# Carried part of a gated recurrence: two 64x64 products per chunk become one 128x128 product on zero-padded states

## What is computed

```python
b = jnp.cumsum(log_f, axis=3)                       # within a chunk
scores = jnp.einsum('bhntd,bhnsd->bhnts', q * jnp.exp(b - b_mid), k * jnp.exp(b_mid - b))
o_intra = jnp.einsum('bhnts,bhnse->bhnte', jnp.where(lower, scores, 0.0), v)
contrib = jnp.einsum('bhnsd,bhnse->bhnde', k * jnp.exp(b_last - b), v)
decay = jnp.exp(b_last[:, :, :, 0, :])
def step(state, inp):
    dec, add = inp
    return dec[..., None] * state + add, state
_, states_in = lax.scan(step, zeros, (decay, contrib))
o_inter = jnp.einsum('bhntd,bhnde->bhnte', q * jnp.exp(b), states_in)
return o_intra + o_inter
```

## Time and profile before

| | |
|---|---|
| Median of 3 runs | 1178.36 us (1177.79 to 1179.91) |
| Profiled execution | 1178.43 us, span from first to last instruction 1176.6 us |
| Busy | PE 99%, PEld 80%, DVE 54%, ACT 38%, POOL 9% |
| Chain that ended last | PE 97%, DVE 1%, ACT 1%, DMA 1% |
| L1414, the carried products | 224 records, 2% of the chain |
| L1040, the scans of states | 8, 1.21 us each |

### The profile page before, as it was taken

One profiled execution on the slowest core, in us unless ns is written; L12 is line 12 of the kernel. 1 busy time (PEld: TensorE's weight loads), 2 busy tenths in 40 slices (PEclk: granted clock), 3 DMA queues, 4 the chain that ended last, 5 costly groups with the idle time before them and its releaser, 6 DMA issues.

```text
span 1176.6 us, 15837 instructions
## 1 busy us (share of the span) xinstructions
PE 1166.8 (99%) x5988; PEld 943.1 (80%) x5988; DVE 636.1 (54%) x768; ACT 445.6 (38%) x650; POOL 100.7 (9%) x82
## 2 busy tenths in 40 slices
PE   9999999999999999999999999999999999999997
PEld 7888888888888777777777778888888888888886
DVE  6755555543334674444599965756455555552223
ACT  6423322322223445455755534444332332231223
POOL 0000000000001210000165510011000000000000
PEclk9999999999999999999999999999999999999999
DMA  6333233233224231111131112422323323323221
GB/s 202 108 107 101 79 105 107 94 132 99 98 78 177 83 124 55 59 67 55 36 108 38 48 61 72 171 98 90 102 95 107 106 77 102 107 80 118 90 90 72
DMA packets 31678, 111.64 MB, mean 95 GB/s; under 512 B 3984, under 2 KB 5136, under 8 KB 31376
## 3 DMA queue, kind: packets, MB, share of 16 engines
q1 hardware_dynamic: 30192, 104.11, 26.5%
q10 hardware_dynamic: 1440, 6.88, 1.6%
HBM read 105.48 MB, written 4.19 MB: 93 GB/s over the span
## 4 chain that ended last, share of the span: by engine, by line
PE 97%; DVE 1%; ACT 1%; DMA 1%; issue 0%; ACTq 0%; SPq 0%; DVEq 0%
PE ps L1124 26%; PE ps L1125 25%; PE ps L1126 25%; PE ps L1160 3%; PE ps L1158 3%; PE ps L1159 3%; PE ps L1414 2%; PE ps L1264 1%; PE ps L1273 1%; PE ps L1289 1%; PE ps L1409 1%; PE ps L1393 1%; PE ps L1374 1%; PE ps L1194 0%; PE ps L1197 0%; DMA raw<-gates_dram 0%
## 5 line engine op out<-in xcount | busy, mean ns | idle before, releaser
L1124 PE MATMUL ps<-h_hi,w_hi 128*128 128x512 f32 x1024 | 407.5, 398 | 0.0
L1126 PE MATMUL ps<-h_hi,w_lo 128*128 128x512 f32 x1024 | 399.0, 390 | 0.0
L1125 PE MATMUL ps<-h_lo,w_hi 128*128 128x512 f32 x1024 | 399.0, 390 | 0.0
L741 DVE TENSOR_TENSOR w_lo<-raw,w_hi 128x1024 fp32r<-128x1024 f32 (+2 forms) x190 | 233.6, 1232 | 193.6 <-ACT w_hi L411 187.9
L411 ACT ACTIVATE w_hi<-raw 128x1024 fp32r<-128x1024 f32 (+1 forms) x182 | 196.2, 1080 | 174.4 <-PE ps L1126 96.1
L1124 PEld LDWEIGHTS ps<-h_hi,w_hi 128*128 128x128 f32 x1024 | 192.2, 188 | 56.0 <-issue 17.0
L1125 PEld LDWEIGHTS ps<-h_lo,w_hi 128*128 128x128 f32 x1024 | 192.3, 188 | 41.3 <-issue 2.9
L1126 PEld LDWEIGHTS ps<-h_hi,w_lo 128*128 128x128 f32 x1024 | 192.2, 188 | 41.0
L481 ACT ACTIVATE g_hi<-un 128x512 f32 (+1 forms) x44 | 27.8, 632 | 250.8 <-DVE un L741 250.8
L741 DVE TENSOR_TENSOR un<-ps,rs 128x512 f32<-128x512 f32 x44 | 30.4, 691 | 122.2 <-PE ps L1126 122.2
L1124 PE MATMUL ps<-g_hi,w_hi 128*128 128x512 f32 x176 | 68.5, 389 | 0.0
(11 more groups left out here) (233 smaller groups left out, 1237.7 us busy)
## 6 DMA issues: line engine op xcount, KB each, us to landing
raw<-up_dram SPq DMA_DIRECT2D x86, 512.0 KB, 3.2
raw<-proj_dram SPq DMA_DIRECT2D x26, 512.0 KB, 3.3
raw<-down_dram SPq DMA_DIRECT2D x16, 704.0 KB, 4.1
raw<-down_dram SPq DMA_DIRECT2D x22, 512.0 KB, 3.2
raw<-gates_dram SPq DMA_DIRECT2D x16, 512.0 KB, 3.2
raw<-branch_dram SPq DMA_DIRECT2D x8, 512.0 KB, 3.3
raw<-wout_dram SPq DMA_DIRECT2D x8, 512.0 KB, 3.2
x_spill_dram<-xT ACTq DMA_DIRECT2D x1, 2048.0 KB, 7.3
```

The lines of the kernel that those rows point to most:

```text
L741: return V.tensor_tensor(out, a, b, op)
L1124: T.matmul(ps[:, bank, :], w_hi[:, slot, cols], moving_hi(j), start=start and j == 0, stop=False)
L1125: T.matmul(ps[:, bank, :], w_hi[:, slot, cols], moving_lo(j), start=False, stop=False)
L1126: ins = T.matmul(ps[:, bank, :], w_lo[:, slot, cols], moving_hi(j), start=False, stop=stop and j == tiles - 1)
```

## The change

The carried product is made for both heads at once. For that each state has 128 columns in place of 64, [128, 128, 8]: rows 0 to 63 hold the first head's state in columns 0 to 63, rows 64 to 127 the second head's in columns 64 to 127, and the rest is zero. The product of such a state with the queries of both heads gives both outputs, one above the other. The zeros are written once, by two memsets of POOL ahead of `to_end(0)`, behind waits for the last silu, the attention's last transposes and products, and the spill. `state[0]` stays in its place and takes the place of the old `state[1]` too, which now lies in tiles 6 and 7 of `xT`. As the two heads' states no longer lie in the same columns, the scan becomes two scans of 64 partitions each, and the waits for `state_done` count two for each unit.

```diff
-        state = [at("state0", 84, [P, HD, NSUP]), at("state1", 86, [P, HD, NSUP])]
+        state = [at("state0", 84, [P, 2 * HD, NSUP])[:], xT[:, 6:8, :].rearrange("p a (e n) -> p (a e) n", n=NSUP)]
...
             key(0)
             key(1)
+            pool.wait_ge(sil_done, HH)
+            pool.wait_ge(pt_done, 2 * ITEMS)
+            pool.wait_ge(pv_done, ITEMS)
+            pool.wait_ge(spilled, 16)
+            for padded in state:
+                nc.gpsimd.memset(padded, 0.0).then_inc(pad_zeroed, 1)
             to_end(0)
...
                 if u >= 2:
-                    act.wait_ge(state_done, u - 1)
+                    act.wait_ge(state_done, 2 * (u - 1))
...
-                con, flat = ps[:, 4 + u % 2, :], state[u % 2][:].rearrange("p e n -> p (e n)")
-                V.tensor_tensor_scan(flat[:, turn], decay[u % 2][:, turn], con[:, turn], 0.0, ALU.mult, ALU.add).then_inc(state_done, 1)
+                con = ps[:, 4 + u % 2, :]
+                if u < 2:
+                    dve.wait_ge(pad_zeroed, 2)
+                for a, rows in enumerate(head_rows):
+                    flat = state[u % 2][rows, HD * a:HD * (a + 1), :].rearrange("p e n -> p (e n)")
+                    V.tensor_tensor_scan(flat[:, turn], decay[u % 2][rows, turn], con[rows, turn], 0.0,
+                                         ALU.mult, ALU.add).then_inc(state_done, 1)
...
-                pe.wait_ge(state_done, u + 1)
+                pe.wait_ge(state_done, 2 * u + 2)
...
-                        for rows in head_rows:
-                            ins = T.matmul(ps[rows, 7, cc], state[d][rows, :, n + 1 if d else n - 1], b_cum[u % 3][rows, cc],
-                                           start=False, stop=d == 1 and n == NSUP - 2)
+                        ins = T.matmul(ps[:, 7, cc], state[d][:, :, n + 1 if d else n - 1], b_cum[u % 3][:, cc],
+                                       start=False, stop=d == 1 and n == NSUP - 2)
```

More of the change, by code:

```diff
@@ L216, in build @@
         o_done, osq_done, oms_done = sem("o_done"), sem("osq_done"), sem("oms_done")
+        pad_zeroed = sem("pad_zeroed")
         oeps_done, or_done, on_done, ybhi_done, yblo_done = (sem(n) for n in (
@@ L229, in build @@
         RAW_CREDIT, W_CREDIT, BANK_CREDIT = RAW_SLOTS, W_SLOTS, 2
+        head_rows = (slice(0, HD), slice(HD, P))
         block = ctx.enter_context(nc.Block())
@@ L1346, in _ @@
                 gate_unit(g)
-            head_rows = (slice(0, HD), slice(HD, P))
             def mean_square(t):
@@ L1389, in contributions @@
                 if u >= 2:
-                    pe.wait_ge(state_done, u - 1)
+                    pe.wait_ge(state_done, 2 * (u - 1))
                 for j in range(ST):
```

## The result

The changed kernel takes 1207.44 us (median; 1206.75 to 1209.81), the kernel before beside it 1178.29: ratio 1.0249, 95% interval 1.0238 to 1.0261. It is slower, as forecast, but by 29.1 us and not by 13.4, and so outside the range that ended at 1194.0. The profiled execution took 1207.81 us, its span is 1205.9.

What follows compares the result with a forecast made beforehand. TensorE (PE), busy for 99% of the span, was taken to bound the kernel. 1178.4 + 13.4 (carried products) + 0 (scans) + 0 (zeroing) = 1191.8 us, range 1183.8 to 1194.0.

Steps and rivals of the forecast that it cites:

- PE bounds, the recurrence has no waits to swallow anything: Recurrence: PE busy for all 109.00 us, one 0.6 us wait from 600 us on; added PE time lengthens the kernel.
- The two heads' products run side by side, so halving the records saves nothing: Carried products in `outputs(u)`: both heads' products start together, so rounds stay 112 and the tempting 10 us is not there.
- A round is the strided load, and it goes by columns: Carried products: the strided load sets the round; 128 columns take it from 0.12 to 0.24 us, +13.4 us.
- Rival (a): Carried products: stride penalty fixed per load, round 0.171 us, +5.7 us, 1184.1 us; chance 0.10.
- rival (b): Carried products: 0.12 us a round already pays for 128 columns; no change, 1178.2 to 1178.9 us; chance 0.10.
- The scans cost nothing: DVE in the recurrence: two 64-row scans add 1.14 us a unit, 9 us in all, but nobody waits; cost 0.
- The cover of -0.04 us at unit 3: Scan to outputs at unit 3: slack if carried products did not get slower, costing some 0 to 0.5 us.
- The zeroing costs nothing: POOL before `to_end(0)`: two memsets run 582.0 to 583.9, ahead of its start at 584.75; cost 0, upper bound 1 us.
- The clock stays up: PE in the recurrence: granted clock, full before, assumed to stay full; the sum had no clock term.
- Rival (c): PE in the 8 outputs: sparser array work halves the clock, adding 30 us, about 1208 to 1222 us; chance 0.02.

Runs made afterwards that it cites:

- the first experiment: Changed kernel with its scans, memsets and padded states, but the carried product made as two 64x64 products: 1178.88 us against 1178.74 for the kernel before, ratio 1.0003.

## Why the prediction was wrong

- **PE bounds, the recurrence has no waits to swallow anything**: right. PE's busy time grew by 28.8 us and the kernel by 29.1.
- **The two heads' products run side by side, so halving the records saves nothing**: right.
- **A round is the strided load, and it goes by columns**: right. 0.235 us was measured where 0.24 was taken; 13.0 us where the sum had 13.4. Load records of 334 ns were forecast as about 340. Rival (a), a fixed penalty, would have had groups of 0.49 and 0.83; rival (b) those of before. The choice against (a) was partly luck: with one width of strided load in the trace, a rate per column and a fixed penalty fit its records equally well. Only the second width decides, (334 - 213)/64 = 1.9 ns for each further column. The Trainium skill, "TensorE: Matmul & The Clock Gate", section "LDWEIGHTS (loading the stationary operand)", counts columns only, an estimated 107 ns for 128; the rounds with steps 1 and 2 are near it (115 and 125 ns), those with 4 and 8 are twice that (230 and 235).
- **The scans cost nothing**: right here, with 64-row scans of 1.22 us. The cover of -0.04 us at unit 3, worked out for fast products, is the 0.2 us wait of the first experiment, at that unit.
- **The zeroing costs nothing**: right, 581.94 to 583.8 as forecast.
- **The clock stays up**: wrong, and this is the failed step. The sum had no term for the clock, and the runs showed one of some 16 us, beside the 13 us of the rounds. Rival (c) had the mechanism, with chance 0.02 and 30 us, and was dismissed with "Nothing in the trace shows it outside the start". (At the start the first matmuls of 512 columns lie 0.43 us apart, 7.40 to 8.25 us for two, though the clock's column reads 1.00 there.) That proves little: the trace of before has no such rounds of a 128x128 product with 64 moving columns under a load of 0.235 us, so it could not show what they do. The range left (c) out on the strength of that. The size in (c) was off too: it priced the outputs themselves at half clock, but the carried products are bound by loads and hardly slow down (1.09 to 1.14 us a group); the cost falls on L1420, L1404 and the first matmuls of the next gate unit. For the first unit it can be read off: 0.26 for L1420, 0.1 for two groups, 0.88 for L1404, and for the six gate matmuls from 618.46 to 621.19 2.73 - 6 x 0.23 = 1.35, less the 0.11 that the first has anyway, together 2.5 us. Eight times that would be 20 us; it is 16, as the sixth and seventh units pay 1.5 to 1.6 each and the eighth nothing. That the measured 1207.44 lies next to (c)'s lower figure of 1208 is luck: that figure is 30 us for the clock and nothing for the rounds.

The causes are shown, not only argued, as far as this: the loss outside the padded product is none (first experiment), the load's part goes with the step of the load (steps 1, 2, 4), the clock's part goes when the same loads have more to move under them (128 columns) and does not come with equally long outputs of small products. Steps 1 and 2 say the same from a third side: the same product with the same 64 columns and a quick load keeps the clock. What stays open is where between these kernels the clock begins to fall, and why the last unit of the changed kernel is spared; neither was looked for.

## What to carry to other kernels

Before products are merged to save records, look in a narrow window of the timeline whether they already run side by side; zeros that are only there to fill the array are loaded at full price. Read the cadence of short products from the starts of neighbouring groups and ask which of load, streaming and issue sets it; here a weight slice that takes every fourth or eighth float32 cost twice a contiguous one in time of a round, and one copy on a free engine can be cheaper. And when a change makes PE wait on loads for longer while it counts as busy, price a fall of the clock as a real case: here its cost landed on the dense work that came next.

## What the runs showed of the hardware

- A strided weight load had two prices, not a slope, over the steps that were run: 128 columns of float32 took 190 ns a record with step 1, 197 with step 2, 330 with step 4 and 334 with step 8, and rounds of about 0.115, 0.125, 0.23 and 0.235 us. With step 8, 64 more columns cost 121 ns more (213 to 334).
- The granted clock fell to 1.2 GHz, seven times, in a stretch in which PE was busy for 137.77 of 138 us. It did so in the changed kernel and with step 4, with 64 moving columns in rounds of 0.23 to 0.235 us, and not with 128 columns under the same loads, nor with 64 in rounds of 0.12 us. Busy time in a profile doesn't say that the clock is safe.
- At 1.2 GHz a group of load-bound carried products took 1.14 us instead of 1.09, and the dense gate matmuls started 0.43 us apart instead of 0.23.
- DVE scans of 64 partitions and of 128 took the same time, 1.22 us.
- ACT took 1.16 us for a copy of 128x512 float32 that reads with a step of 8 elements, and 0.59 us for its copy of the same size from PSUM.
